# Reading the expert rows back in twelve transfers of the loads' queue, with the gate weights behind the first tile

## The reference, cut to what matters

```python
# top 4 of 32 experts for each token, weights from a softmax over the four logits
x = x + sum_k w_k * expert_k(rmsnorm(x, g_ffn))          # clamped SwiGLU, 1024 -> 1024 -> 1024
x = x + (p_i @ w_ple_proj) * sigmoid(rmsnorm(x, g_ple) @ w_ple_gate)   # p_i: 256 wide
y = rmsnorm(x, g_final)
```

## Time and profile before

| | us |
|---|---|
| median of 3 runs | 1362.52 (1360.78 to 1362.62) |
| the profiled execution's own time | 1358.81 |
| its span | 1357.0 |
| last scatter issued | 1280.29 |
| read-back issued | 1286.83 |
| first gate matmul | 1307.47 |

### The profile page before, as it was taken

One profiled execution on the slowest core, in us unless ns is written; L12 is line 12 of the kernel. 1 busy time (PEld: TensorE's weight loads), 2 busy tenths in 40 slices (PEclk: granted clock), 3 DMA queues, 4 the chain that ended last, 5 costly groups with the idle time before them and its releaser, 6 DMA issues.

```text
span 1357.0 us, 15632 instructions
## 1 busy us (share of the span) xinstructions
PE 1205.2 (89%) x5919; PEld 494.9 (36%) x5919; DVE 308.6 (23%) x849; ACT 180.7 (13%) x416; POOL 77.5 (6%) x146
## 2 busy tenths in 40 slices
PE   5999979989999988889888888989988898998856
PEld 4565655533333332233333232333332233333322
DVE  2333555331111111111111111111111111111153
ACT  2232432110001000000000000010000001000122
POOL 6000101000000000000000000000000000000000
PEclk9999987989999999999999999999999999999978
DMA  9560157288999999999999999999999999999941
GB/s 291 182 170 16 51 188 292 94 359 361 429 428 428 429 429 428 428 429 428 429 429 428 429 428 429 428 428 428 429 429 429 428 428 429 429 428 428 358 146 39
DMA packets 64555, 478.88 MB, mean 353 GB/s; under 512 B 9136, under 2 KB 26136, under 8 KB 38100
## 3 DMA queue, kind: packets, MB, share of 16 engines
q1 hardware_dynamic: 57968, 462.19, 82.4%
q0 software_dynamic: 4496, 16.02, 3.3%
q10 hardware_dynamic: 2068, 0.37, 0.2%
HBM read 469.32 MB, written 14.47 MB: 357 GB/s over the span
## 4 chain that ended last, share of the span: by engine, by line
DMA 57%; PE 38%; DVE 2%; ACT 1%; issue 1%; POOL 0%; SPq 0%; ACTq 0%; POOLq 0%; DVEq 0%
DMA ring<-in_w_up 55%; PE ps L752 35%; PE ps L764 1%; DMA ring<-expert_rows 1%; DMA X<-in_x_sample 0%; DMA expert_rows<-area,rowi 0%; DVE X L1438 0%; PE ps L861 0%; PE ps L863 0%; PE ps L1006 0%; PE ps L892 0%; PE ps L1088 0%; ACT H L587 0%; DVE area L1152 0%; ACT area L702 0%
## 5 line engine op out<-in xcount | busy, mean ns | idle before, releaser
L752 PE MATMUL ps<-ring,area 128*64 128x512 f32 x3232 | 728.0, 597 | 93.5 <-DMA ring<-in_w_up 77.0
L752 PEld LDWEIGHTS ps<-ring,area 128*64 128x64 f32 x3232 | 221.8, 137 | 556.4 <-issue 383.8
L1382 DVE TENSOR_SCALAR area<-ps 128x512 f32<-128x512 f32 x34 | 23.5, 692 | 429.5 <-PE ps L752 429.5
L752 PE MATMUL ps<-ring,hT 128*128 128x512 f32 (+2 forms) x320 | 109.6, 566 | 2.8 <-issue 2.3
L752 PE MATMUL ps<-H,area 128*64 128x512 f32 (+1 forms) x420 | 103.2, 609 | 2.5 <-DVE area L1356 2.5
L554 POOL DMA_INDIRECT expert_rows<-area,rowi x34 | 33.2, 977 | 979.9 <-ACT area L705 979.9
L1386 DVE TENSOR_SCALAR area<-ps 128x512 f32<-128x512 f32 x34 | 23.5, 692 | 259.7 <-PE ps L752 259.7
L752 PE MATMUL ps<-area 128*64 128x1 f32 (+6 forms) x756 | 79.0, 285 | 1.7 <-issue 1.2
L752 PE MATMUL ps<-hT,ring 128*128 128x320 f32 x256 | 74.9, 448 | 0.0
L694 ACT ACTIVATE area<-ps 128x512 f32<-128x512 f32 x35 | 20.9, 597 | 393.6 <-PE ps L752 393.6
L752 PEld LDWEIGHTS ps<-ring,hT 128*128 128x128 f32 (+1 forms) x320 | 46.4, 174 | 60.9 <-issue 57.9
(11 more groups left out here) (193 smaller groups left out, 547.8 us busy)
## 6 DMA issues: line engine op xcount, KB each, us to landing
ring<-in_w_up SPq DMA_DIRECT2D x68, 2048.0 KB, 25.8
ring<-in_w_down SPq DMA_DIRECT2D x68, 2048.0 KB, 22.6
ring<-in_w_gate SPq DMA_DIRECT2D x66, 2048.0 KB, 25.2
ring<-in_w_in SPq DMA_DIRECT2D x16, 512.0 KB, 8.6
ring<-in_w_in SPq DMA_DIRECT2D x2, 2048.0 KB, 9.5
ring<-in_w_o SPq DMA_DIRECT2D x2, 2048.0 KB, 15.6
early<-in_w_gate SPq DMA_DIRECT2D x2, 2048.0 KB, 18.9
ring<-in_w_ple_gate SPq DMA_DIRECT2D x1, 4096.0 KB, 31.6
```

Source lines behind the costliest of these rows:

```text
L752: return T.matmul(out, lhsT, rhs, start=first, stop=last)
L1382: V.tensor_scalar(gate, ps[:, G_BANK, :], LIMIT, None, ALU.min).then_inc(g_sb, 1)
```

## The change

POOL's three read-backs are gone. SP now waits for `y_dma` to count all scatters, and issues the read-back itself, one transfer for each tile and choice: 4 of 512 KB for tile 0, 4 of 512 KB for tile 1, 4 of 256 KB for tile 2. The gate weights, which SP issued as soon as slot 1 was free, are issued behind tile 0's four. Every transfer of the read-back has its own semaphore, and `combine` waits for each choice by itself.

```diff
-        yg = [sem(f"yg{i}") for i in range(NT)]
+        yg = [[sem(f"yg{i}_{k}") for k in range(TOPK)] for i in range(NT)]
...
             wait_used((n1, 0), 1)
-            sp.dma_start(wple, A["w_ple_gate"][0].rearrange("(c p) n -> p c n", p=P)).then_inc(tail_in[0], 16)
+
+            sp.wait_ge(y_dma, n1 * 16 + 16)
+            for t in range(NT):
+                r = ROWS[t]
+                src = yscr[2 * t * P * TOPK:2 * (t * P + r) * TOPK, :].rearrange("(p k h) n -> p k (h n)", k=TOPK, h=2)
+                for k in range(TOPK):
+                    sp.dma_start(Yg[t][0:r, k, :], src[:, k, :]).then_inc(yg[t][k], 16)
+                if t == 0:
+                    sp.dma_start(wple, A["w_ple_gate"][0].rearrange("(c p) n -> p c n", p=P)).then_inc(tail_in[0], 16)
...
-            for t in range(NT):
-                r = ROWS[t]
-                g.dma_start(Yg[t][0:r, :, :],
-                            yscr[2 * t * P * TOPK:2 * (t * P + r) * TOPK, :].rearrange("(p k h) n -> p k (h n)", k=TOPK, h=2)).then_inc(yg[t], 16)
...
             def combine(t):
                 r = ROWS[t]
-                dve.wait_ge(yg[t], 16)
                 for k in range(TOPK):
+                    dve.wait_ge(yg[t][k], 16)
                     ins = V.scalar_tensor_tensor(X[0:r, t, :], Yg[t][0:r, k, :], w4[0:r, t, k:k + 1], X[0:r, t, :], ALU.mult, ALU.add)
```

## The result

The changed kernel takes 1358.54 us (median of 20 runs, 1354.27 to 1361.60); the kernel before, run beside it, 1360.80 (20 runs, 1358.13 to 1364.79). The ratio over all these runs is 0.9975, with a 95% interval of 0.9964 to 0.9986: 3.4 us faster, interval 1.9 to 4.9. The prediction gave 0.60 to a change that can't be told from none; what came is faster by more, to which it gave 0.30. The time lies in the range.

What follows compares the result with a forecast made beforehand. The tail bounds the kernel, with gate weights arriving last: -5.6 (tile 0) +2.0 (gate weights) +0.7 (tile 1's rows) +1.1 (its `hT`) is -1.8 us; with 0.4 for the clock -2.2, giving 1360.3 us, range 1358.2 to 1363.0.

Steps and rivals of the forecast that it cites:

- What bounds the end after the change: In the tail: gate weights arrive last, tile 1 follows behind them, and ACT's order delays tile 1's `hT`.
- The three waits of PE: PE waits for gate weights (about 1299.5 to 1303.9), tile 1's scaled rows (0.6 us) and tile 1's `hT` (1.1 us).
- The scatter: Last scatter before the read-back: 0.5 us less than its 5.81 from issue to landing, range 0 to 1.
- The gate weights: Queued behind tile 0's choices: 6.29 MB together, 15.3 us at 412 GB/s plus 2.9 us, landing at 1303.85.
- Tile 1: Behind the gate weights: DVE combines it without a wait, ending at 1310.4, 2.1 us later than before.
- L: Time at which the gate weights land in the tail: forecast 1303.85, bounds 1302.7 and 1305.9.
- The sum: End of the profiled span: -5.6 tile 0, +2.0 gate weights, +0.7 tile 1's rows, +1.1 its `hT`, making -1.8 us.
- The clock's 0.4 us: PE's first half of tile 0: a late clock rise hidden in PE's new waits, counted as 0.4 us gained against a median.
- straggling: Slower rival: the gate weights' traffic ends spread out, L moves by 3.7 to 1307.6, end +1.9 us; over +2.7: chance 0.07.
- serial service: Slower rival: short read-back transfers served one after another, tile 0 landing at 1300.2, end about 17 us later; chance 0.03.
- The gate weights and the scatter at their good bounds: Faster rival: gate weights land at 1302.7, end -3.0 us, -3.4 with the clock, 1359.1; chance 0.29 for past -2.7.
- A fixed cost for each transfer: Tile 0's read-back: 2.0 us paid per choice would land it after 12.8 us; the prediction argued queued transfers follow without gap.

Runs made afterwards that it cites:

- e5: Changed kernel with ACT's squares of tile 2 moved behind the copies of tile 1's transposes; one profile, tail 73.5 us against the changed kernel's 74.7.
- e4: Changed kernel with gate weights in two halves, the first behind tile 0's choices, the second behind tile 1's; ratio 0.9951 to the kernel before.
- e2: Changed kernel with the gate weights issued early, where the kernel before had them, the twelve transfers kept; ratio 0.9968 to the kernel before.
- e6: Changed kernel with the gate weights' first half issued early at their old place, the second half behind tile 1; ratio 0.9964 to the kernel before.
- e7: Changed kernel with both edits, gate weights in two late halves and ACT's squares of tile 2 moved later; ratio 0.9952 to the kernel before.

## Why the prediction was wrong in its size, by its own steps

*What bounds the end after the change: right.* The gate weights last, then tile 1 behind them, then ACT's order. The three waits of PE, e5 (the order of ACT) and e4 (the place behind 4 MB) show it.

*The scatter: this step failed.* The prediction took 0.5 us off its 5.81, range 0 to 1, "near its row". It measured 3.55 less. The prediction had the right bound in hand, "a small landing from idle, 3.3 us, so 2.5 us less at most", and even that was too high a floor. It chose the row before over the bound because the DMA engines were only 0.54 busy on the mean. But the gate weights landed at 1288.4, two us after the scatter had, and the share of busy engines fell slowly (DMA share and GB/s last):

```profile
1285.00:1286.00 1.00, 1.00 (x4) 0.44 (x3) 0.00 (x0) 0.67 (x1) 0.00 (x0) 1.00 0.37 148
1286.00:1287.00 1.00, 1.00 (x3) 0.38 (x2) 0.00 (x0) 0.00 (x0) 0.17 (x1) 1.00 0.22 90
1287.00:1288.00 1.00, 1.00 (x4) 0.22 (x2) 0.00 (x0) 0.00 (x0) 1.00 (x2) 1.00 0.10 41
```

So some engines were done with the gate weights while others were not, and the mean hides those that are behind. The reading that fits is that the scatter has landed only when the latest engine has done its part; no run shows it engine by engine. What 4, 2 and 0 MB in the queue do to it (5.8, 3.2, 2.3) was measured; why it costs this much was not.

*The gate weights: a little short.* From SP's first issue to their landing 18.2 us were forecast (2.9 over the bytes, 15.3 for the bytes), 18.6 measured (1287.70 to 1306.3).

*Tile 1: short by 0.7.* Its fourth choice was forecast at L + 5.1, in time for DVE. It came at about L + 5.9; DVE waited 0.83 us for it, and ended at L + 7.3 instead of L + 6.55. Between 1311 and 1312 the engines moved 193 GB/s, about the rate of tile 2's 64 rows, which suggests that tile 2's choices were already moving beside it; no run separates the two. From there to `hT` the forecast 11.7 us were 11.7.

*The sum.* Forecast -1.8 in the profile. With -3.05 for the scatter, +0.4 for the gate weights, +0.7 for tile 1, and +0.3 since PE took 33.3 us and not 33.0 from tile 1's first half to the end, it is -3.4, as measured.

*The clock's 0.4 us:* not shown. PE's first half took 8.5 us after and 8.8 before, and since the wait for tile 1's rows stands behind it, those 0.3 us didn't reach the end. How the clock varies over executions of one kernel no run shows. Over the eleven profiles the first half took 8.5 to 10.0 us, so the prediction was right that this can cost more than here: e2, e6 and e7, whose PE has no wait behind it, pay it in full.

*The rivals.* No straggling: the gate weights' excess over their bytes was 3.3 us. No serial service: tile 0's four choices were used within 5.7 us of one another. "The gate weights and the scatter at their good bounds" is the case that came, by the scatter alone, and beyond its bound: L was put at 1302.7 and came at 1301.2.

*A fixed cost for each transfer:* it did not add up over queued ones, as the prediction argued. DVE used tile 0's fourth choice 8.5 us after SP's first issue, not after 12.8. The Trainium skill gives the figure of 2.0 us plus the bytes at 436 GB/s in "DMA: Bandwidth & Descriptors", section Anatomy of one DMA — SWDGE (gpsimd) path, as a fit for each transfer of POOL's queue.

## What to carry to other kernels

A transfer that waits for nobody still has a price where it lies: 4 MB of prefetch with 19 us of slack added 3.5 us to a small scatter on the chain that had to pass the same 16 engines. Before moving it, ask what then stands behind it: here the same 4 MB, moved whole, brought tile 0's combination 3.2 us forward and put tile 1's 4.9 us back (the changed kernel beside e2), and moved in two halves, each ahead of its first use, it kept the first without the second. And follow a late arrival through every engine's fixed order: that ACT took tile 2's squares ahead of tile 1's copy cost another 1.3 us, by the profiles. Last, where variants differ by a microsecond or two, look at the granted clock of each before giving the difference to the change.

## What the runs showed of the hardware that was not expected

- The last scatter, by POOL's queue, landed in 2.3 us on idle DMA engines, in 3.2 behind 2 MB and in 5.7 to 5.8 behind 4 MB of SP's loads, although in the kernel before the engines were on the mean only 0.54 busy.
- POOL's and SP's queues shared the engines by packets: with 106 packets against 104, POOL's rows of 16 KB took 1.70 of 2.13 MB beside SP's rows of 4 KB.
- The split cost no bandwidth that shows: the gate weights, queued behind four transfers of 512 KB, landed within 0.4 us of what the bytes and one fixed cost give.
- After an idle stretch at a granted clock of 0.50, PE's clock rose to 1.00 between 2.8 and 5.8 us after its first gate matmul, and the same 16 matmuls took 8.5 to 10.0 us.
